# Hybrid decoder block on one core: the test of the largest load is taken early, and the common case follows it

## The chip, the core and the metric

The kernel runs on one core of a Trainium2 chip. The metric is the device time of one execution in microseconds, the median of several runs. The engines are named as in the profile: PE (TensorE) multiplies matrices into PSUM, DVE (VectorE) and ACT (ScalarE) work on vectors, POOL (GpSimd) gathers rows and copies small columns, and SP (SyncE) issues nearly all transfers. Each engine runs its own program; they meet at semaphores.

## The reference

A batch of one with T = 512 tokens of width 1024 goes through one decoder block: a norm, two token mixers (retention and mLSTM) with their projections, an output projection and a residual add, then a hierarchical mixture of experts, a residual add and a last norm. The part around the change is the mixture of experts:

```python
g_w, g_idx = lax.top_k(group_prob, 1)
sel_logits = e_logits[jnp.arange(T), g_idx[:, 0]]
top_logits, e_idx = lax.top_k(sel_logits, TOP_K)          # 2 of the 8 experts of the best of 4 groups
expert_id = g_idx * EXPERTS_PER_GROUP + e_idx             # 32 experts
...
def expert_block(args):
    xb, e = args
    return (jax.nn.silu(xb @ w_gate[e]) * (xb @ w_up[e])) @ w_down[e]
...
return rms_norm(x, norm_final_w)
```

w_gate and w_up are 1024 x 512 and w_down is 512 x 1024 for each expert, all in float32: 6 MB an expert, 192 MB in all. Every weight is read once.

## The kernel before

**Mixer.** The projections are 22 blocks of 512 columns, each of four mix pairs (two slices of 128 rows of the weight), 88 mix pairs in all. ScalarE and VectorE split each weight into a head and a tail (wh, wl, rings of four), and TensorE makes three products of them at line 463. The last two blocks (B_WO) add into the stream x2.

**Router.** After the last block TensorE turns x2 into h2T (turn_stream) and makes the logits (line 608); VectorE picks the experts, and TensorE counts each token's place within its expert (line 624). Then come the tables of moe_round: at16 and at_slot (lines 1449 and 1450) say which token sits in which slot of an expert, the product at line 723 makes the token table (tok_tab), and the product at line 733 the weights by slot (slot_tab, its columns 1 and 2).

**Experts.** The experts are worked on as 16 pairs (PAIRS). One expert has CAP = 64 slots, so that a pair fills the 128 partitions. A pair is: gather its 128 token rows from DRAM (POOL, line 1559, into xg), turn them (turn_x, line 429, then x_copy on VectorE), gate product and up product (gate_or_up, line 650, in two halves each), sigmoid on ScalarE (line 1014), two multiplications on VectorE (lines 1414 and 1419), turn the result (turn_h), down product (down, line 676, two halves), split into yh and yl, and add into x2 by one-hot products (combine, lines 686 and 687, and line 1403). The combine of a pair is spread over the next pair.

**Weights.** A pair's weights come in PAIR_CHUNKS = 12 chunks of 1 MB (gate 4, up 4, down 4), 192 chunks in all, into MOE_RAW = 18 buffers raw_moe, whose places overlay those of the mixer. moe_chunk on SP issues one: after the first 18 it waits until the chunk four before it has landed (IN_FLIGHT, line 360) and until the chunk 18 before it has been used (line 365 for an early half). Chunks 0 to 7 go out during the last mixer blocks, chunks 8 to 15 after the stream's stores (line 400), chunks 16 and 17 after the logits.

**Rounds.** If an expert has more than 64 tokens, further rounds over all pairs are needed. VectorE writes the largest count and the number of extra rounds to cnt. Every engine does pairs 0 to 14 of round 0, then reads cnt, goes through a loop of seven rounds whose body stands in an If and is not taken here, and then does the last pair, number 15 (last_pair(extra) on PE; on SP the last 12 chunks, from LAST_CHUNKS on). On SP it reads

```python
            round_chunks(0)
            sp.wait_ge(cnt_ok, 1)
            most = sp.value_load(cnt[0:1, 0:1], min_val=0, max_val=T)
            with sp.Fori(1, ROUNDS, 1) as r:
                with sp.If(most > r * CAP):
                    round_chunks(r)
            extra = sp.value_load(cnt[0:1, 1:2], min_val=0, max_val=ROUNDS - 1)
            for m in range(LAST_CHUNKS, R_CHUNKS):
                moe_chunk(m, extra, 0, True)
```

at lines 408 to 416. After the last pair come its combine (line 1485 on VectorE), the squares, the last norm (line 1490) and four stores of the output.

Of the kernel before, what the change touches and what calls it, by code (L numbers as in the profile page):

```python
# [68 lines left out]
LAST_CHUNKS = R_CHUNKS - PAIR_CHUNKS  # L69
SP_LOOPS = (LAST_CHUNKS - MOE_RAW) // (2 * MOE_RAW)  # L70
# [23 lines left out]
def hybrid_block(nc, x, norm_mix_w, w_in, ret_gn_w, w_ret, conv_w, conv_b, b_i, b_f, mlstm_gn_w, w_mlstm, w_out,  # L94
                 norm_ffn_w, w_group, b_group, w_router, b_router, w_gate, w_up, w_down, norm_final_w, consts, out):
    ctx = ExitStack()
    with ctx:
# [6 lines left out]
        def sem(name):  # L104
# [27 lines left out]
                   enumerate([64, 72, 0, 8, 16, 24, 80, 88, 32, 40, 48, 56, 96, 104, 112, 120, 144.5, 152.5])]  # L132
# [9 lines left out]
        h2T = at("h2T", 144.5, [P, KD, T])  # L142
# [12 lines left out]
        squares = at("squares", 168.5, [P, TT, D])  # L155
# [19 lines left out]
        def small(name, shape, dt=F32):  # L175
# [64 lines left out]
        at_ok = sem("slots_ready")  # L240
# [21 lines left out]
            "one_hot_ready", "table_in_psum", "table_ready", "counts_ready"))  # L262
# [40 lines left out]
        def _(sp):  # L303
# [72 lines left out]
            def round_chunks(r):  # L376
                if not isinstance(r, int):
                    for m in range(LAST_CHUNKS, R_CHUNKS):
                        moe_chunk(m, r - 1, 0, True)
# [5 lines left out]
                for m in range(MOE_RAW + SP_LOOPS * 2 * MOE_RAW, LAST_CHUNKS):  # L385
                    moe_chunk(m, r, 0, True)
# [27 lines left out]
            extra = sp.value_load(cnt[0:1, 1:2], min_val=0, max_val=ROUNDS - 1)  # L414
            for m in range(LAST_CHUNKS, R_CHUNKS):
                moe_chunk(m, extra, 0, True)
# [9 lines left out]
        def _(pe):  # L426
# [211 lines left out]
            def gate_or_up(r, i, n, up, half):  # L638
# [4 lines left out]
                if half == 0 and (not isinstance(N, int) or N > 0):  # L643
# [19 lines left out]
            def down(r, i, n, half):  # L663

                N, m = r * PAIRS + i * LOOP_PAIRS + n, PAIR_CHUNKS * n + 8 + 2 * half
                if half == 0:
                    pe.wait_ge(hf_ok, N + 1)
                    if not isinstance(N, int) or N > 0:
                        pe.wait_ge(yl_ok, N * 2)
# [44 lines left out]
            def moe_round(r):  # L714
                N0 = r * PAIRS
                if not isinstance(r, int):
                    last_pair(r - 1)
                    combine(N0 - 1, range(8))
# [8 lines left out]

                pe.wait_ge(at_ok, r + 1)
                pe.wait_ge(ww_ok, 1)
                for n in range(2 * TT):  # L730
# [6 lines left out]
                turn_x(N0, 0)  # L737
                turn_x(N0, 1)
                for half in range(2):
                    gate_or_up(r, 0, 0, 0, half)  # L740
                for half in range(2):
                    gate_or_up(r, 0, 0, 1, half)
                turn_x(N0 + 1, 0)
                turn_h(N0)
                down(r, 0, 0, 0)
                turn_x(N0 + 1, 1)
                down(r, 0, 0, 1)
# [32 lines left out]
            N = extra * PAIRS + (PAIRS - 1)  # L780
            pe.wait_ge(c_add, N * 8 + 2)
            pe.wait_ge(oh_ok, N + 1)
            for g in range(8):
                if g < 2:
                    pe.wait_ge(yl_ok, N * 2 + (g + 1))
                    pe.sem_inc(pe_past, 1)
                if g >= 4:
                    pe.wait_ge(fadd, g - 3)
                product((cb[:, 2, :], cb[:, 3, :], pj[:, 0, :], pj[:, 1, :])[g % 4], g).then_inc(fc_ps, 1)
# [3 lines left out]
        def _(act):  # L793
# [191 lines left out]
            def square(t):  # L985
                act.wait_ge(free[t], BLOCKS)
                nc.scalar.activation(squares[:, t, :], x2[:, t, :], ACT.Square, accum_out=ssq[:, t:t + 1]).then_inc(sq_ok, 1)
# [19 lines left out]
            act.wait_ge(e2_ok, 1)  # L1007
            nc.scalar.activation(stat[:, 1, 0:TT], rt[:, 6, 0:TT], ACT.Sigmoid)
# [16 lines left out]
            def moe_round(r):  # L1025
                N0 = r * PAIRS
                if not isinstance(r, int):
                    pair(N0 - 1, last=True)
                pair(N0, first=isinstance(r, int))
                with act.Fori(0, PAIRS - 2, 1) as i:  # L1030
                    pair(N0 + i + 1)

            moe_round(0)
# [22 lines left out]
        def _(dve):  # L1056
# [354 lines left out]
            def pair(N, first=False, last=False, bare=False):  # L1411
# [16 lines left out]
                if first:  # L1428
                    dve.wait_ge(ir_in, 16)
# [6 lines left out]
            def moe_round(r):  # L1436
                N0 = r * PAIRS
                if not isinstance(r, int):

                    pair(N0 - 1, last=True)  # L1440
                    add(N0 - 1, range(8))
# [8 lines left out]
                V.tensor_tensor(at_slot[:, :, :, :].rearrange("p k t s -> p (k t) s"), where, slots, ALU.is_equal).then_inc(at_ok, 1)  # L1450
                if isinstance(r, int):
                    own(V.reduce_max(rt[:, 7, 40:41], cb[:, 1, TT * NE:(TT + 1) * NE], AX.X))
                dve.wait_ge(tab_ps, r * 2 + 2)
                V.tensor_scalar(tok_tab[:, :], cb[:, 2, 0:PAIRS], float(NO_TOKEN), None, ALU.add).then_inc(tab_ok, 1)
                if isinstance(r, int):
                    weights()
                    V.tensor_copy(cnt[:, 0:1], rt[0:1, 7, 40:41])
                    own(V.tensor_scalar(rt[0:1, 7, 48:48 + ROUNDS - 1], kc[0:1, K_LIMIT:K_LIMIT + ROUNDS - 1], rt[0:1, 7, 40:41], None, ALU.is_lt))
                    own(V.reduce_sum(rt[0:1, 7, 41:42], rt[0:1, 7, 48:48 + ROUNDS - 1], AX.X))
                    V.tensor_copy(cnt[:, 1:2], rt[0:1, 7, 41:42]).then_inc(cnt_ok, 1)  # L1460
                V.tensor_scalar(slot_tab[:, :, 0], cb[:, 2, 0:PAIRS], float(NO_TOKEN), None, ALU.add)
                dve.wait_ge(wt_ps, r * 2 + 2)
                V.tensor_copy(slot_tab[:, :, 1:3].rearrange("p n c -> p c n"), cb[:, 3, 0:NE].rearrange("p (c n) -> p c n", c=2)).then_inc(wt_ok, 1)
# [3 lines left out]
                pair(N0, first=isinstance(r, int), bare=True)  # L1467
                with dve.Fori(0, PAIRS - 2, 1) as i:
                    pair(N0 + i + 1)

            moe_round(0)
# [22 lines left out]
        def _(pool):  # L1494
# [52 lines left out]
            def gather(N, n, copies=0):  # L1547

                if not isinstance(N, int) or N > 0:
# [12 lines left out]
            def columns(N, n):  # L1562

                if not isinstance(N, int) or N > 0:
# [5 lines left out]
            def moe_round(r):  # L1570
                N0 = r * PAIRS
                if not isinstance(r, int):
                    columns(N0 - 1, PAIRS - 1)
                pool.wait_ge(tab_ok, r + 1)
                gather(N0, 0)
                gather(N0 + 1, 1)
                pool.wait_ge(wt_ok, r + 1)
                columns(N0, 0)
# [4 lines left out]
            moe_round(0)  # L1583
# [60 lines left out]
```

## Time and profile before

| | |
|---|---|
| median of 3 runs | 1086.86 us (1086.61 to 1087.71) |
| the profiled execution | 1088.14 us, of which the span is 1086.4 |
| mean granted TensorE clock | 0.978 of full |
| busy time: PE, DVE, ACT, POOL | 1013.1, 425.0, 276.6, 70.4 us |
| moved | 263.83 MB, 243 GB/s in the mean |

All positions in the text are microseconds from the start of the span. The page cuts the span into 40 slices of 27.16 us; a stretch view gives for chosen stretches the busy time, the granted clock (1.00 is 2.4 GHz and 0.50 is 1.2 GHz) and the bytes moved. A timeline row gives the start and the length of a group of instructions, and in square brackets how long the engine had been idle and what ended that. The chain of waits is followed back from the last instruction; "issue" in it is time in which the engine waited for nothing that the profile shows. Ends of matmuls are modelled, so a busy TensorE is not one at its peak. SPq is SyncE's queue.

### The profile page before, as it was taken

The page shows a single profiled execution, that of the slowest core. Times are in us where ns is not written, and L with a number is a line of the kernel's source. Part 1 is how long each engine was busy: PE and PEld are TensorE (multiplying, and loading weights), DVE is VectorE, ACT ScalarE, POOL GpSimd, SP SyncE. Part 2 cuts the span into 40 slices and gives each one's busy share as a digit, 9 for nine tenths or more (in the row PEclk, how much of TensorE's full clock was granted, in tenths as well). Part 3 has the DMA queues.
Part 4 walks back from the last instruction along what each step waited for, and adds up shares of the span by engine and source line. Part 5 has one row for each costly group of instructions (what it writes and reads, how often), then busy time and mean ns, then how long its engine had stood idle before and what let it go on. Part 6 is the DMA issues. An engine that isn't in the chain of part 4 may idle for free.

```text
span 1086.4 us, 12967 instructions
## 1 busy us (share of the span) xinstructions
PE 1013.1 (93%) x4661; PEld 649.7 (60%) x4661; DVE 425.0 (39%) x733; ACT 276.6 (25%) x462; POOL 70.4 (6%) x102
## 2 busy tenths in 40 slices
PE   4999999999999999999993999999999999889874
PEld 4888888888888888888883333333333333333322
DVE  4236356434533334535524123333333232333316
ACT  5343564433333336413221000000000000000002
POOL 0564000000000000000000000000000000000000
PEclk9999999999999999999995999999999999999978
DMA  7313222222222222245829799999999999999791
GB/s 273 116 55 141 78 78 78 78 78 78 78 78 78 93 101 79 77 127 171 328 109 395 303 421 420 420 421 421 421 421 420 420 417 421 421 420 418 303 383 78
DMA packets 59959, 263.83 MB, mean 243 GB/s; under 512 B 9152, under 2 KB 9216, under 8 KB 35208
## 3 DMA queue, kind: packets, MB, share of 16 engines
q1 hardware_dynamic: 57432, 257.94, 60.2%
q0 software_dynamic: 2480, 5.26, 1.3%
q8 instruction: 30, 0.49, 0.2%
q14 instruction: 17, 0.14, 0.0%
HBM read 263.17 MB, written 4.20 MB: 246 GB/s over the span
## 4 chain that ended last, share of the span: by engine, by line
PE 55%; DMA 39%; issue 2%; DVE 2%; SPq 1%; ACT 0%; DVEq 0%; POOLq 0%; ACTq 0%
PE pj L463 45%; DMA raw_moe<-in_w_gate_dram 13%; DMA raw_moe<-in_w_up_dram 13%; DMA raw_moe<-in_w_down_dram 12%; PE pj L650 2%; PE cb L429 2%; DMA xg<-x_scratch,tok_tab 1%; PE cb L608 1%; PE cb L482 1%; PE pj L676 1%; PE cb L508 1%; DMA vrow<-in_mlstm_conv_w_dram 1%; PE cb L550 1%; PE cb L512 0%; PE cb L515 0%
## 5 line engine op out<-in xcount | busy, mean ns | idle before, releaser
L650 PE MATMUL pj<-raw_moe,xT 128*64 128x512 f32 x1024 | 233.0, 604 | 25.2 <-issue 10.2
L1070 DVE TENSOR_TENSOR wl<-raw_mix,wh 128x1024 fp32r<-128x1024 f32 x88 | 109.1, 1245 | 183.3 <-ACT wh L807 183.0
L650 PEld LDWEIGHTS pj<-raw_moe,xT 128*64 128x64 f32 x1024 | 75.1, 139 | 168.0 <-issue 168.0
L463 PE MATMUL pj<-wh,hTh 128*128 128x512 f32 x320 | 130.1, 407 | 1.6 <-DVE hTl L1098 1.6
L463 PE MATMUL pj<-wl,hTh 128*128 128x512 f32 x320 | 125.3, 392 | 0.0
L463 PE MATMUL pj<-wh,hTl 128*128 128x512 f32 x320 | 125.0, 391 | 0.0
L807 ACT ACTIVATE wh<-raw_mix 128x1024 fp32r<-128x1024 f32 x88 | 92.4, 1057 | 121.9 <-PE pj L463 111.1
L1403 DVE TENSOR_TENSOR x<-x,cb 128x512 f32<-128x512 f32 x120 | 77.0, 683 | 103.7 <-PE cb L687 103.7
L676 PE MATMUL pj<-raw_moe,hf 128*64 128x512 f32 x512 | 116.7, 598 | 0.8 <-ACT hf L1018 0.8
L463 PE MATMUL pj<-hTh,wh 128*128 128x512 f32 x192 | 80.2, 418 | 0.0
L463 PE MATMUL pj<-hTh,wl 128*128 128x512 f32 x192 | 75.4, 393 | 0.0
L463 PE MATMUL pj<-hTl,wh 128*128 128x512 f32 x192 | 75.1, 391 | 0.0
L676 PEld LDWEIGHTS pj<-raw_moe,hf 128*64 128x64 f32 x512 | 34.2, 136 | 67.0 <-issue 66.8
L463 PEld LDWEIGHTS pj<-wh,hTh 128*128 128x128 f32 x320 | 60.2, 188 | 13.7 <-issue 2.1
L463 PEld LDWEIGHTS pj<-wl,hTh 128*128 128x128 f32 x320 | 60.1, 188 | 13.0
L463 PEld LDWEIGHTS pj<-wh,hTl 128*128 128x128 f32 x320 | 60.3, 188 | 11.8
L1023 ACT ACTIVATE yh<-pj,now 128x512 fp32r<-128x512 f32 x32 | 20.4, 684 | 159.6 <-PE cb L687 143.6
L686 PE MATMUL cb<-yh,hot 128*128 128x512 f32 x124 | 55.0, 444 | 1.3 <-DVE yl L1433 0.8
L1414 DVE SCALAR_TENSOR_TENSOR sg<-pj,now,sg 128x512 f32<-128x512 f32 x16 | 12.0, 751 | 110.0 <-ACT sg L1014 110.0
L687 PE MATMUL cb<-yl,hot 128*128 128x512 f32 x124 | 49.2, 397 | 0.0
L1018 ACT ACTIVATE hf<-cb 128x512 f32<-128x512 f32 x16 | 9.6, 597 | 151.7 <-PE cb L429 151.7
L1408 DVE TENSOR_TENSOR xT<-cb,nwc 128x512 f32<-128x512 f32 x32 | 22.0, 689 | 60.6 <-PE cb L429 60.6
(274 smaller groups left out, 1217.4 us busy)
## 6 DMA issues: line engine op xcount, KB each, us to landing
raw_moe<-in_w_gate_dram SPq DMA_DIRECT2D x64, 1024.0 KB, 9.7
raw_moe<-in_w_up_dram SPq DMA_DIRECT2D x64, 1024.0 KB, 10.1
raw_moe<-in_w_down_dram SPq DMA_DIRECT2D x64, 1024.0 KB, 9.7
raw_mix<-in_w_in_dram SPq DMA_DIRECT2D x32, 1024.0 KB, 5.0
raw_mix<-in_w_ret_branch_dram SPq DMA_DIRECT2D x4, 1024.0 KB, 5.1
raw_mix<-in_w_mlstm_branch_dram SPq DMA_DIRECT2D x4, 1024.0 KB, 5.6
raw_mix<-in_w_out_dram SPq DMA_DIRECT2D x4, 1024.0 KB, 5.2
xt<-in_x_dram SPq DMA_DIRECT2D x4, 512.0 KB, 5.2
```

The source lines that it names most:

```text
L429: return nc.tensor.transpose(o, i, kc[0:k, K_IDENT:K_IDENT + k])
L463: m = nc.tensor.matmul(pj[:, i, :], lhsT, rhs, start=k == 0 and n == 0, stop=k == KD - 1 and n == 2)
L650: mm = nc.tensor.matmul(pj[a * CAP:(a + 1) * CAP, up, :], xT[:, 4 * half + k, a * CAP:(a + 1) * CAP], raw_moe[(m + a) % MOE_RAW][:, k, :], ...
L676: mm = nc.tensor.matmul(pj[a * CAP:(a + 1) * CAP, 2 + c, :], hf[:, 2 * half + f, a * CAP:(a + 1) * CAP], raw_moe[(m + a) % MOE_RAW][:, 2 * ...
L686: nc.tensor.matmul(bank, hot[:, t * P:(t + 1) * P], yh[:, c * 512:(c + 1) * 512], start=True, stop=False)
L687: return nc.tensor.matmul(bank, hot[:, t * P:(t + 1) * P], yl[:, c * 512:(c + 1) * 512], start=False, stop=True)
L807: nc.scalar.activation(wh[:, q % RING, :, :], raw_mix[n % MIX_RAW][:, 2 * (q % 2):2 * (q % 2) + 2, :], ACT.Copy).then_inc(wh_ok, 1)
L1023: nc.scalar.activation(yh[:, c * 512:(c + 1) * 512], pj[:, 2 + c, :], ACT.Copy, scale=now[:, 1:2]).then_inc(yh_ok, 1)
L1070: V.tensor_tensor(wl[:, q % RING, :, :], raw_mix[n % MIX_RAW][:, 2 * (q % 2):2 * (q % 2) + 2, :], wh[:, q % RING, :, :].bitcast(F32), ALU. ...
L1403: V.tensor_tensor(part, part, cb[:, 2 + g % 2, :], ALU.add).then_inc(c_add, 1)
L1408: V.tensor_tensor(xT[:, ks, :], cb[:, part, :].rearrange("p (k n) -> p k n", k=4), nwc[:, ks].unsqueeze(2).to_broadcast([P, 4, P]), ALU.mu ...
L1414: V.scalar_tensor_tensor(sg[:, :], pj[:, 0, :], now[:, 2:3], sg[:, :], ALU.mult, ALU.mult).then_inc(q_ok, 1)
```

## The change

- On every engine all 16 pairs of a round stand together (all_pairs), and the test of the largest count stands ahead of the pairs of round 0: on PE after the token table, the first gather's transposes and the first gate product (first_gate); on DVE after the tables and xT of pair 0; on POOL after the first gather; on ACT ahead of everything of the pairs. On SP all 192 chunks of round 0 are issued first and its test follows them.
- On PE the test is an If with an Else. The common case (largest count at most 64) follows the test at once, with the last sum; further rounds stand in the Else. ACT, DVE and POOL keep the loop of seven rounds with an If, ahead of the last all_pairs(extra).
- cnt is signalled in two steps: the largest count (cnt_ok) ahead of the token table, the number of extra rounds (rounds_ok) after it.
- The weights' table (at_slot, weights(), line 733) comes after the token table and, on PE, after the first gate product and the test.
- The buffers raw_moe are in another order. Chunks 8 and 9 take places of the mixer's raw weights (free once the last tail is made), chunks 10 and 11 places of wh and wl (free after mix pair 85), and all four are issued ahead of the stream's stores. Chunks 12 to 17 follow the stores, without the wait for the logits. h2T moves to 168.5, and squares becomes two tiles of [P, D], with a wait of a square for the one two before it.
- ACT loads the sigmoid table after its test instead of after the router.

```diff
@@ SP @@
+            sp.wait_ge(wl_ok, MIX_PAIRS)
+            moe_chunk(8, 0, 0, False)
+            moe_chunk(9, 0, 0, False)
+            wait_mix_pair(sp, MIX_PAIRS - 3)
+            moe_chunk(10, 0, 0, False)
+            moe_chunk(11, 0, 0, False)
             for t in range(TT):
                 sp.wait_ge(free[t], BLOCKS)
                 sp.dma_start(x_dram[t * P:(t + 1) * P, :], x2[:, t, :]).then_inc(st_in, 16)
-            for m in range(8, 16):
+            for m in range(12, MOE_RAW):
                 moe_chunk(m, 0, 0, False)
...
-            sp.wait_ge(lg_ps, 1)
-            for m in range(16, MOE_RAW):
-                moe_chunk(m, 0, 0, False)
             round_chunks(0)
             sp.wait_ge(cnt_ok, 1)
...
-            extra = sp.value_load(cnt[0:1, 1:2], min_val=0, max_val=ROUNDS - 1)
-            for m in range(LAST_CHUNKS, R_CHUNKS):
-                moe_chunk(m, extra, 0, True)
@@ PE @@
-            moe_round(0)
+            token_table(0)
+            first_gate(0)
             pe.wait_ge(cnt_ok, 1)
             most = pe.value_load(cnt[0:1, 0:1], min_val=0, max_val=T)
-            with pe.Fori(1, ROUNDS, 1) as r:
-                with pe.If(most > r * CAP):
-                    moe_round(r)
-
-            extra = pe.value_load(cnt[0:1, 1:2], min_val=0, max_val=ROUNDS - 1)
-            last_pair(extra)
...
+            with pe.If(most < CAP + 1):
+
+                all_pairs(0)
+                last_sum(PAIRS - 1)
+            with pe.Else():
+                with pe.Fori(1, ROUNDS, 1) as r:
+                    with pe.If(most > r * CAP):
+                        all_pairs(r - 1)
+                        combine(r * PAIRS - 1, range(8))
+                        token_table(r)
+                        first_gate(r)
+                pe.wait_ge(rounds_ok, 1)
+                extra = pe.value_load(cnt[0:1, 1:2], min_val=0, max_val=ROUNDS - 1)
+                all_pairs(extra)
+                last_sum(extra * PAIRS + (PAIRS - 1))
@@ ACT @@
             with act.Fori(1, ROUNDS, 1) as r:
                 with act.If(most > r * CAP):
-                    moe_round(r)
-
-
+                    all_pairs(r - 1)
+            nc.scalar.activation(stat[:, 1, 0:TT], onesq[:, 0:TT], ACT.Sigmoid)
+
+            act.wait_ge(rounds_ok, 1)
             extra = act.value_load(cnt[0:1, 1:2], min_val=0, max_val=ROUNDS - 1)
-            pair(extra * PAIRS + (PAIRS - 1), last=True)
+            all_pairs(extra)
@@ DVE @@
+            tables(0)
+            dve.wait_ge(ir_in, 16)
             most = dve.value_load(cnt[0:1, 0:1], min_val=0, max_val=T)
             with dve.Fori(1, ROUNDS, 1) as r:
                 with dve.If(most > r * CAP):
-                    moe_round(r)
-
+                    all_pairs(r - 1)
+                    add(r * PAIRS - 1, range(8))
+                    tables(r)
 
             extra = dve.value_load(cnt[0:1, 1:2], min_val=0, max_val=ROUNDS - 1)
-            pair(extra * PAIRS + (PAIRS - 1), last=True)
+            all_pairs(extra)
@@ POOL @@
+            first_gather(0)
             pool.wait_ge(cnt_ok, 1)
             most = pool.value_load(cnt[0:1, 0:1], min_val=0, max_val=T)
             with pool.Fori(1, ROUNDS, 1) as r:
                 with pool.If(most > r * CAP):
-                    moe_round(r)
+                    all_pairs(r - 1)
+                    first_gather(r)
+            pool.wait_ge(rounds_ok, 1)
             extra = pool.value_load(cnt[0:1, 1:2], min_val=0, max_val=ROUNDS - 1)
-            columns(extra * PAIRS + (PAIRS - 1), PAIRS - 1)
+            all_pairs(extra)
```

## Rows read from the trace of the kernel before

**Rows 1.** The page, section 2: bytes moved in each of 40 slices.

```profile
GB/s 273 116 55 141 78 78 78 78 78 78 78 78 78 93 101 79 77 127 171 328 109 395 303 421 420 420 421 421 421 421 420 420 417 421 421 420 418 303 383 78
```

**Rows 2.** Experts, 630 to 1000: one stretch (PE busy, clock, DMA, GB/s), then SyncE's waits.

```profile
630.00:1000.00 370.00, 355.47 (x1598) 1.00 1.01 420
...
SPq L360 <- DMA raw_moe<-in_w_gate_dram: 100.4, 51, 2.8
```

**Rows 3.** Stretches around the second hole, columns as in rows 2.

```profile
1017.00:1027.00 10.00, 9.83 (x49) 1.00 0.31 108
1025.00:1027.00 2.00, 2.00 (x12) 1.00 0.43 78
...
1027.00:1056.00 29.00, 18.81 (x74) 0.76 1.01 420
...
1039.27:1045.00 5.73, 5.73 (x14) 0.50 1.01 422
```

**Rows 4.** The chain of waits around SyncE's test: start, length, what.

```profile
1013.42 0.49 SPq L410
...
1014.46 5.26 issue
...
1020.24 0.20 issue
...
1024.07 0.29 SPq L414
...
1025.02 0.35 SPq L373
...
1033.64 5.63 issue
```

**Rows 5.** Timeline of TensorE, pairs 14 and 15.

```profile
1003.18 3.65 PE L650 MATMUL pj<-raw_moe,xT 128*64 128x512 f32 x16 [1.58 <-DMA raw_moe<-in_w_gate_dram]
...
1012.98 3.65 PE L650 MATMUL pj<-raw_moe,xT 128*64 128x512 f32 x16
...
1028.68 0.40 PE L687 MATMUL cb<-yl,hot 128*128 128x512 f32 x1
1039.27 13.39 PE L650 MATMUL pj<-raw_moe,xT 128*64 128x512 f32 x48 [10.19 <-issue]
...
1053.72 3.65 PE L650 MATMUL pj<-raw_moe,xT 128*64 128x512 f32 x16
...
1061.74 7.09 PE L676 MATMUL pj<-raw_moe,hf 128*64 128x512 f32 x32
```

**Rows 6.** The chain of waits ahead of the first pair.

```profile
588.28 8.65 DMA xg<-x_scratch,tok_tab
...
599.04 4.82 PE pj L650 x16
...
604.12 0.36 SPq L373
```

**Rows 7.** Stretches around the first hole, columns as in rows 2.

```profile
585.00:597.00 12.00, 2.52 (x48) 0.50 0.94 380
597.00:606.00 9.00, 8.91 (x36) 0.76 0.16 40
```

**Rows 8.** The gathers, issue to landing: all (view of xg), then the first two (page).

```profile
DMA to landing us min/median/max: 3.3/8.3/8.7
...
xg<-x_scratch,tok_tab POOLq DMA_INDIRECT x2, 6.0
```

**Rows 9.** Timeline of PE, ACT and DVE: slot table, pair 0 and pair 15.

```profile
589.22 1.93 PE L733 MATMUL cb<-wrhot,at_slot 128*64 128x32 f32 x32 [2.27 <-DVE wrhot L1391]
...
607.38 0.69 ACT L1014 ACTIVATE sg<-pj,now 128x512 f32<-128x512 f32 x1 [23.32 <-PE pj L650]
...
1049.29 0.69 ACT L1014 ACTIVATE sg<-pj,now 128x512 f32<-128x512 f32 x1 [18.91 <-PE pj L650]
...
1050.08 0.75 DVE L1414 SCALAR_TENSOR_TENSOR sg<-pj,now,sg 128x512 f32<-128x512 f32 x1 [18.43 <-ACT sg L1014]
```

More of the change, by code:

```diff
@@ L141, in hybrid_block @@
         raw_mix = [at(f"raw_mix{s}", 144.5 + 8 * s, [P, 4, 512]) for s in range(MIX_RAW)]
-        h2T = at("h2T", 144.5, [P, KD, T])
+        h2T = at("h2T", 168.5, [P, KD, T])
         irow = at("irow", 160.5, [P, T])
@@ L154, in hybrid_block @@
         sgm = at("sgm", 168.5, [P, KD, T])
-        squares = at("squares", 168.5, [P, TT, D])
+        squares = [at("squares_even", 184.5, [P, D]), at("squares_odd", 162.5, [P, D])]
         xT = at("xT", 168.5, [P, KD, P])
@@ L384, in round_chunks @@
                         moe_chunk(m, r, i, True)
-                for m in range(MOE_RAW + SP_LOOPS * 2 * MOE_RAW, LAST_CHUNKS):
+                for m in range(MOE_RAW + SP_LOOPS * 2 * MOE_RAW, R_CHUNKS):
                     moe_chunk(m, r, 0, True)
@@ L636, in turn_x, with gate_or_up @@
                 m.then_inc(xT_ps, 1)
-            def gate_or_up(r, i, n, up, half):
+            def gate_or_up(r, i, n, up, half, first=False):
                 N, m = r * PAIRS + i * LOOP_PAIRS + n, PAIR_CHUNKS * n + 4 * up + 2 * half
@@ L642, in gate_or_up @@
                     pe.wait_ge(xT_ok, N * 2 + (half + 1))
-                if half == 0 and (not isinstance(N, int) or N > 0):
+                if half == 0 and not first:
                     pe.wait_ge((q_ok, h_ok)[up], N)
@@ L661, in turn_h, with down @@
                 m.then_inc(ht_ps, 1)
-            def down(r, i, n, half):
+            def down(r, i, n, half, first=False):
                 N, m = r * PAIRS + i * LOOP_PAIRS + n, PAIR_CHUNKS * n + 8 + 2 * half
@@ L667, in down @@
                     pe.wait_ge(hf_ok, N + 1)
-                    if not isinstance(N, int) or N > 0:
+                    if not first:
                         pe.wait_ge(yl_ok, N * 2)
@@ L712, in last_pair, with token_table @@
                 down(r, 0, n, 1)
[L714 to L718, printed above, removed]
+            def token_table(r):
                 pe.wait_ge(hot_ok, r + 1)
@@ L736, in moe_round, with first_gate, all_pairs @@
                             m.then_inc(wt_ps, 1)
-                turn_x(N0, 0)
-                turn_x(N0, 1)
+            def first_gate(r):
+                turn_x(r * PAIRS, 0)
+                turn_x(r * PAIRS, 1)
                 for half in range(2):
-                    gate_or_up(r, 0, 0, 0, half)
+                    gate_or_up(r, 0, 0, 0, half, first=True)
+            def all_pairs(r):
+                N0 = r * PAIRS
+                slot_table(r)
                 for half in range(2):
-                    gate_or_up(r, 0, 0, 1, half)
+                    gate_or_up(r, 0, 0, 1, half, first=True)
                 turn_x(N0 + 1, 0)
                 turn_h(N0)
-                down(r, 0, 0, 0)
+                down(r, 0, 0, 0, first=True)
                 turn_x(N0 + 1, 1)
-                down(r, 0, 0, 1)
+                down(r, 0, 0, 1, first=True)
                 def pair(i, n):
@@ L769, in moe_round, with last_sum @@
                     pair(0, n)
-            moe_round(0)
+                last_pair(r)
+            def last_sum(N):
+                pe.wait_ge(c_add, N * 8 + 2)
+                pe.wait_ge(oh_ok, N + 1)
+                for g in range(8):
+                    if g < 2:
+                        pe.wait_ge(yl_ok, N * 2 + (g + 1))
+                        pe.sem_inc(pe_past, 1)
+                    if g >= 4:
+                        pe.wait_ge(fadd, g - 3)
+                    product((cb[:, 2, :], cb[:, 3, :], pj[:, 0, :], pj[:, 1, :])[g % 4], g).then_inc(fc_ps, 1)
+            token_table(0)
+            first_gate(0)
             pe.wait_ge(cnt_ok, 1)
             most = pe.value_load(cnt[0:1, 0:1], min_val=0, max_val=T)
-            with pe.Fori(1, ROUNDS, 1) as r:
-                with pe.If(most > r * CAP):
-                    moe_round(r)
-            extra = pe.value_load(cnt[0:1, 1:2], min_val=0, max_val=ROUNDS - 1)
-            last_pair(extra)
[L780 to L789, printed above, removed]
+            with pe.If(most < CAP + 1):
[12 more added lines that the diff above has]
+                last_sum(extra * PAIRS + (PAIRS - 1))
         @block.scalar
@@ L1023, in pair, with all_pairs @@
                     nc.scalar.activation(yh[:, c * 512:(c + 1) * 512], pj[:, 2 + c, :], ACT.Copy, scale=now[:, 1:2]).then_inc(yh_ok, 1)
-            def moe_round(r):
+            def all_pairs(r):
                 N0 = r * PAIRS
-                if not isinstance(r, int):
-                    pair(N0 - 1, last=True)
-                pair(N0, first=isinstance(r, int))
+                pair(N0, first=True)
                 with act.Fori(0, PAIRS - 2, 1) as i:
                     pair(N0 + i + 1)
-            moe_round(0)
+                pair(N0 + (PAIRS - 1), last=True)
             act.wait_ge(cnt_ok, 1)
@@ L1409, in x_copy, with pair @@
                                 ALU.mult).then_inc(xT_ok, 1)
-            def pair(N, first=False, last=False, bare=False):
+            def pair(N, last=False, bare=False):
                 dve.wait_ge(now_ok, N + 1)
@@ L1434, in pair, with tables @@
                                            ALU.mult, ALU.subtract).then_inc(yl_ok, 1)
-            def moe_round(r):
+            def tables(r):
                 N0 = r * PAIRS
                 if not isinstance(r, int):
-                    pair(N0 - 1, last=True)
-                    add(N0 - 1, range(8))
                     dve.wait_ge(it_ok, r)
@@ L1449, in moe_round @@
                 V.tensor_tensor(at16[:, :, :, :].rearrange("p k t s -> p (k t) s"), where, slots, ALU.is_equal).then_inc(hot_ok, 1)
-                V.tensor_tensor(at_slot[:, :, :, :].rearrange("p k t s -> p (k t) s"), where, slots, ALU.is_equal).then_inc(at_ok, 1)
                 if isinstance(r, int):
                     own(V.reduce_max(rt[:, 7, 40:41], cb[:, 1, TT * NE:(TT + 1) * NE], AX.X))
+                    V.tensor_copy(cnt[:, 0:1], rt[0:1, 7, 40:41]).then_inc(cnt_ok, 1)
                 dve.wait_ge(tab_ps, r * 2 + 2)
@@ L1545, in _, with gather @@
             pool.wait_ge(zero_ok, 4)
-            def gather(N, n, copies=0):
-                if not isinstance(N, int) or N > 0:
+            def gather(N, n, copies=0, first=False):
+                if not first:
                     pool.wait_ge(xT_ps, N * 2)
@@ L1560, in gather, with columns @@
                                         bounds_check=T - 1, oob_is_err=False).then_inc(gat, 16)
-            def columns(N, n):
-                if not isinstance(N, int) or N > 0:
+            def columns(N, n, first=False):
+                if not first:
                     pool.wait_ge(yl_ok, N * 2)
@@ L1568, in columns, with first_gather, all_pairs @@
                 pool.tensor_copy(now[:, :].unsqueeze(1), slot_tab[:, col, :]).then_inc(now_ok, 1)
-            def moe_round(r):
+            def first_gather(r):
+                pool.wait_ge(tab_ok, r + 1)
+                gather(r * PAIRS, 0, first=True)
+            def all_pairs(r):
                 N0 = r * PAIRS
[L1572 to L1575, printed above, removed]
                 gather(N0 + 1, 1)
                 pool.wait_ge(wt_ok, r + 1)
-                columns(N0, 0)
+                columns(N0, 0, first=True)
                 with pool.Fori(0, PAIRS - 2, 1) as i:
@@ L1581, in moe_round @@
                     columns(N0 + i + 1, i + 1)
-            moe_round(0)
+                columns(N0 + (PAIRS - 1), PAIRS - 1)
+            first_gather(0)
             pool.wait_ge(cnt_ok, 1)
```

38 lines of the change are left out of this document (19 added, 19 removed).

## The prediction, made before the change was run

> **What bounds the kernel now.** I read the page in slices first, then the transfers, then the chain of waits at both ends of the expert stage, and last the order of the engines there. The slice row says that from about 605 us on the core moves 420 GB/s nearly without a break, with one dent in the slice that begins at 1005 us [rows 1]. From 630 to 1000 us the mean is 420 GB/s, and what SyncE's queue waits for there is an earlier weight transfer, not TensorE [rows 2]. So the expert stage is paced by 192 chunks of 1 MB, 18 of them loaded ahead; TensorE keeps up and sits waiting for a chunk before parts of the late pairs [rows 5]. The last instruction can move only if the transfers start earlier, run without a hole, or what follows them gets shorter.
>
> There are two holes. From 597 to 606 us the rate is 40 GB/s: the 18 buffers are full, and nothing has been consumed. The chain there is the first gather (8.65 us), its transposes, the first half of a gate product, and only then the nineteenth chunk at 604.12 [rows 6]. The second hole is from 1017 to 1027 us, 108 GB/s against 420 [rows 3]: 10 x (420 - 108) / 420 = 7.4 us of transfer time are lost. It is SyncE's own. At 1013.42 it turns from the chunks to the load test, and its next chunk goes out at 1025.02 [rows 4]. Of the 11.6 us between, one step of 5.26 us is the first jump over the loop's untaken body; later rounds jump in 0.20 us. TensorE does the same test: its last product of pair 14 starts at 1028.68 and takes 0.40, chunks for pair 15 are there at 1033.64, yet it starts at 1039.27 [rows 4, 5], and it then runs at half clock, granted 0.50 of full (1.2 GHz), until about 1045 [rows 3].
>
> **The change, tail part.** SyncE now issues all 192 chunks and tests afterwards; TensorE tests after its first gate product, so pair 15 follows pair 14 with nothing between. The best measure of such a hand-over is pair 14 itself. Its second gate half starts at 1003.18, as its chunks land [rows 5]. Twelve chunks later means 12 x 1.049 MB / 420 GB/s = 30.0 us, so that pair 15's second gate half starts at 1033.1. (No gather is left in that stretch; with one the period is nearer 30.7, which I keep for the range.) From there to the last up half it is 9.8 us, as in pair 14 (1003.18 to 1012.98). From the last up half to the down product pair 15 takes 1061.74 - 1053.72 = 8.0 us, the same code and combines as before. So the down product starts at 1033.1 + 9.8 + 8.0 = 1050.9 instead of 1061.74. Is its data there? The transfers ended at about 1056.5 and lose the hole of 7.4: 1049.1, in time. Behind the down product nothing changes: 1061.74 to the end of the span, 24.7 us. Gain 10.9 us. The half clock goes with the idle time that preceded it and is within this difference, not on top of it. What is late next is the landing of the last pair's first chunks: TensorE loses the gap and the slow products, but it cannot run ahead of the stream. SyncE's test moves behind its last issue, near 1043, and lasts until about 1055; it is next wanted at the first store, near 1067.
>
> **The front part.** Chunks 8 to 11 move to buffers that are free during the last mixer blocks, when the transfers stand still, and chunks 16 and 17 no longer wait for the logits. Before, ten chunks follow the stream's stores, and the stream is busy until about 596 (the rate of 380 GB/s from 585 to 597 is 11 us at full rate) [rows 7]; four chunks fewer take 4.19 MB / 420 GB/s = 10.0 us from it, so it ends near 586. The gather is issued at 588.28 [rows 6]. In the trace the first gather, into a busy stream, took 8.65 us; its twin, issued at 599.88 into the empty stretch, is the minimum of 3.3 us, since the two of that kind have a median of 6.0 [rows 8] and (8.65 + 3.3) / 2 = 6.0. So I take 3.35: everything after the gather moves 5.3 us earlier, the first gate product from 599.04 to 593.7 and the first refill from 604.12 to 598.8. The bounds are 0 (the gather stays at 8.65) and 5.3. When the gather is issued I leave as it is: VectorE drops at_slot ahead of the token table, but it waits for the table's product anyway.
>
> What is added between the first gate product and the first up product: TensorE's test and the slot table, which stood at 589.22 in idle time, 1.93 us [rows 9]. The trace has no test on TensorE whose start shows. SyncE's, without the jump, is 1013.42 to 1014.46 = 1.04 us [rows 4]; the bounds are 0, hidden behind queued matmuls, and 6.3 with the jump's 5.26. I take 1.04, because the common case is now the code behind the test. Gates then end 8.1 us after their start (599.04 to about 607.1, ahead of the sigmoid at 607.38 [rows 9]), at 601.8; up begins at 604.8 and frees two chunks 3.6 us later, at 608.4. The stream has had four chunks since 600.4 (traffic begins some 1.6 us after the issue, as from 604.12 on) and would run dry at 610.4; with 1.1 us from issue to traffic (1025.02 [rows 4], then a busy share of 0.43 up to 1027 [rows 3]) it has 0.9 us to spare. Cost 0.
>
> VectorE, ScalarE and GpSimd each run the loop of seven untaken branches before pair 0 instead of before pair 15. Bound from SyncE's row, 10.65 us; above it ScalarE's and VectorE's late loops can be no longer than their idle time before 1049 to 1050 (18.9 and 18.4 us [rows 9]), so I take 10.65 and keep 18. ScalarE: 587 to 598, a table load, then ready; its sigmoid is due near 607. GpSimd: the second gather goes out near 601 instead of 594.6, lands by 609, is wanted near 612. VectorE is the tight one: xT copied at 594.5, loop until 605.7 with its last load, then the weight columns and GpSimd's copy of one, both small, for which I allow 1 us, the sigmoid 0.69 and the first multiplication 0.75 [rows 9], ready near 608; the up product ends near 612. Some 3 to 4 us spare, and two more before the stream notices. The other moved pieces (h2T, two small squares tiles with one wait for a square two back, an early sigmoid table) have no consumer near.
>
> **Sum.** 1086.4 - 10.9 - 5.3 = 1070.2 us of span. The profiled execution was 1088.14, 1.74 over its span, and 1.28 over the median of the runs; 1086.86 - 16.2 = 1070.7.
>
> **Rivals.** (a) TensorE's test costs the 5.26 us of a jump after all: up is freed 5.26 us later, less 0.9 of spare: 1075.1. For it: the code behind the test is new to TensorE. Against it: it is the next in line, and no straight stretch in the late pairs shows such a gap. (b) The gather gains nothing, because its 8.65 us were not the stream's doing or because the preload runs on: 1086.86 - 10.9 = 1076.0. Against it stands the twin of 3.3.
> (c) Slower than before: the early loop on VectorE (or GpSimd) pays the first jump's 5.26 us in every round. The absorbed part is 5 us; six more such jumps are 31.6, so 26.6 are lost on the front and the result is 1070.7 + 26.6 = 1097.3. It decides from the second dear jump upward; four more (21 us) eat the whole gain. For it: the loops of these three engines are nowhere visible, and they are exposed only now. Against it: SyncE's loop shows one dear jump only, TensorE's whole gap of 10.2 us [rows 5] has no room for two and the rest, and an all-dear loop (36.8 us) doesn't fit into the 18.4 us that VectorE had.
> What SyncE's row shows is one slow jump, then fast ones. The Trainium skill (Runtime: NRT & Kernel Launch, section Instruction fetch mechanics) says that "a taken branch whose target isn't in the current 2-page window forces a DMA fetch of the target page". By that rule a loop whose head or tail lies across a page edge would refetch in every round, which is the mechanism of (c), and 1097 its price; by SyncE's rows it fetches once. Whether an edge falls so is not to be seen before.
> (d) The change doesn't do what it says at the tail: the last pair's chunks come in time but SyncE's longer straight run or TensorE paces them otherwise, and only the front gains: 1086.86 - 5.3 = 1081.6.
>
> **Chances.** Forecast 0.62, (a) 0.13, (b) 0.12, (c) 0.08, (d) 0.03, and 0.02 for (c) with about four dear jumps, where it comes out even. The range: below, 1067.5, for a first gate half at full clock (2.4 GHz) instead of half and a test that is hidden; above, 1078, past (a) and (b) and a tail period of 30.7. Left out are (c), (d) and a little of the rest. Within 0.2% is about what a measurement of this kernel can tell from no change: faster 0.90, same 0.02, slower 0.08.
>
> **What would show it.** The stream without a dent between 1000 us and its end; the first gather near 3.3 us and the preload over before it is issued; the nineteenth chunk near 599; TensorE at full clock through the last pair, its down product near 1045 or 1046 (1050.9 - 5.3); the last chunk landing near 1044. Wrong would be: a gap of over 3 us between the first gate and the first up product, a hole in the stream near 610, TensorE waiting for VectorE's first inner product, or ScalarE's first sigmoid after 609.

## The result and the profile after

The changed kernel takes 1073.86 us (median of 4 runs, 1071.89 to 1074.01) against 1087.28 us (4 runs, 1086.61 to 1087.78): a ratio of 0.9873 with a 95% interval of 0.9856 to 0.9890. That is 13.4 us faster; forecast were 16.2 and 1070.7 us, with a range of 1067.5 to 1078. The profiled executions are 1088.14 and 1073.83 us, their spans 1086.4 and 1072.0, 14.4 apart. Most of the difference between 13.4 and 14.4 is that the profiled execution of before lay 0.86 us above the median of the four runs, and that of the changed kernel 0.03 below.

First the page of the changed kernel, the span and the bytes moved in 40 slices, which answers to [rows 1]; then stretches (PE busy, clock, DMA share, GB/s) at both holes, which answer to [rows 3, 7].

```profile
span 1072.0 us, 12923 instructions
...
GB/s 276 118 43 156 79 79 79 79 79 79 79 79 79 79 81 116 79 80 167 358 194 336 247 420 419 420 422 421 420 420 421 420 417 421 422 420 420 416 414 91
```

```profile
585.00:597.00 12.00, 4.79 (x30) 0.50 0.12 34
597.00:606.00 9.00, 9.00 (x69) 0.93 0.59 210
...
1000.00:1020.00 20.00, 18.49 (x86) 1.00 1.01 413
1020.00:1040.00 20.00, 18.36 (x80) 1.00 1.01 422
...
1044.00:1046.00 2.00, 1.73 (x7) 1.00 0.62 250
```

The second hole is gone: 413 and 422 GB/s where there were 108, and the granted clock is 1.00 through the last pair. The stream thins out between 1044 and 1046 us, about where its last chunk was forecast (1044). In front the stretch from 585 to 597 us, in which the stream moved 380 GB/s, is now nearly empty (34): the preload is over when the gather is issued, and the idle stretch has moved ahead of it rather than vanished. The chain of waits there answers to [rows 6], start, length, what:

```profile
588.20 4.45 DMA xg<-x_scratch,tok_tab
...
592.79 1.96 PE cb L426 x8
594.77 8.80 PE pj L647 x32
```

And the timelines, in the order SyncE, TensorE, ScalarE, GpSimd and VectorE at the front, then TensorE in the last pair, which answer to [rows 5, 9]:

```profile
600.39 1.07 SPq L372 DMA_DIRECT2D raw_moe<-in_w_up_dram  x2
...
603.35 1.08 PE L728 MATMUL cb<-wrhot,at_slot 128*64 128x32 f32 x32
604.25 7.08 PE L647 MATMUL pj<-raw_moe,xT 128*64 128x512 f32 x32
...
590.49 1.28 ACT L1050 ACT_TABLE_LOAD   x1 [7.95 <-issue]
...
595.62 1.00 POOL L1572 DMA_INDIRECT xg<-x_scratch,tok_tab  x1 [5.99 <-PE cb L426]
...
604.50 0.20 DVE L1476 COPY slot_tab<-cb 128x32 f32<-128x32 f32 x1 [9.02 <-PE cb L728]
605.98 0.75 DVE L1426 SCALAR_TENSOR_TENSOR sg<-pj,now,sg 128x512 f32<-128x512 f32 x1 [1.28 <-ACT sg L1027]
...
1029.01 3.65 PE L647 MATMUL pj<-raw_moe,xT 128*64 128x512 f32 x16 [0.31 <-DMA raw_moe<-in_w_gate_dram]
1033.99 3.65 PE L647 MATMUL pj<-raw_moe,xT 128*64 128x512 f32 x16 [1.32 <-DMA raw_moe<-in_w_up_dram]
...
1038.80 3.65 PE L647 MATMUL pj<-raw_moe,xT 128*64 128x512 f32 x16
...
1046.79 7.09 PE L673 MATMUL pj<-raw_moe,hf 128*64 128x512 f32 x32
```

The first refill goes out at 600.39 instead of 604.12, 3.7 us earlier. The down product of the last pair starts at 1046.79 instead of 1061.74, 14.95 us earlier, so the tail gave 11.2 of them. The span ends 14.4 us earlier; 0.6 us were given back by the last store alone, for which SyncE's queue waited 2.4 us before and 3.0 us after.

### The profile page after: what moved, and what is told of

Same layout as the page of the kernel before. It is cut to its first block, busy times and chain, and to the rows that moved or that the text cites. A ratio compares the mean times of both kernels' runs of the same rounds, so it can differ in the third digit from the quotient of the medians.

```text
span 1072.0 us, 12923 instructions
## 1 busy us (share of the span) xinstructions
PE 1010.2 (94%) x4661; PEld 647.8 (60%) x4661; DVE 425.0 (40%) x733; ACT 276.6 (26%) x462; POOL 70.7 (7%) x102
## 4 chain that ended last, share of the span: by engine, by line
PE 55%; DMA 40%; DVE 2%; issue 1%; SPq 1%; ACT 0%; DVEq 0%; POOLq 0%
PE pj L460 45%; DMA raw_moe<-in_w_up_dram 13%; DMA raw_moe<-in_w_down_dram 13%; DMA raw_moe<-in_w_gate_dram 13%; PE cb L426 2%; PE pj L647 2%; PE cb L605 1%; PE cb L479 1%; PE pj L673 1%; PE cb L505 1%; DMA vrow<-in_mlstm_conv_w_dram 1%; PE cb L547 1%; PE cb L512 0%; PE cb L509 0%; PE cb L486 0%
```

## The experiments

The comparisons are with the changed kernel's 1073.86 us, and each group of runs had the kernel before beside it (medians 1087.49, 1087.71, 1086.98 and 1087.74 us).

**The preload undone.** The order of the buffers, the issues of chunks 8 to 17, h2T and squares as in the kernel before.

```diff
-                   enumerate([64, 72, 0, 8, 16, 24, 80, 88, 144.5, 152.5, 96, 112, 32, 40, 48, 56, 104, 120])]
+                   enumerate([64, 72, 0, 8, 16, 24, 80, 88, 32, 40, 48, 56, 96, 104, 112, 120, 144.5, 152.5])]
...
-            for m in range(12, MOE_RAW):
+            for m in range(8, 16):
                 moe_chunk(m, 0, 0, False)
```

> The changed kernel with the old order of the buffers and the old preload (chunks 8 to 15 after the stream's stores, 16 and 17 after the logits). Theory: the front gain comes from the gather meeting an empty stream; it is back at about 8.6 us, the nineteenth chunk goes out some 4 us later, 1077.9 us (1077 to 1079). Rival: the gather is faster for another reason (the order of the tables and of the products), and the preload is beside the point: 1073.9.

Measured: 1077.62 us (1077.29 to 1078.21). The chain has the long gather again:

```profile
588.86 8.73 DMA xg<-x_scratch,tok_tab
```

So the front is worth 3.8 us, and it comes by the gather meeting an empty stream. The order of the tables and of the products, which this kernel keeps, does not shorten the gather.

**The preload alone, in the kernel before.** The same lines the other way round.

> The kernel before with the new buffers, the new preload, h2T and squares moved, and nothing else. Theory: only the front gain, 1087.3 - 4.0 = 1083.3 us, gather 3.7 to 4.5. The slot table stands here again ahead of the gather. If its activity is what let TensorE's clock rise earlier, the first gate half up to the first refill takes 5.1 us as in the kernel before, not 5.6 as in the changed one. Rival: nothing is gained without the early test, 1087.3.

Measured: 1082.76 us (1082.20 to 1083.29), ratio 0.9956 with an interval of 0.9940 to 0.9973, so 4.7 us. Chain of waits of this kernel:

```profile
588.69 4.13 DMA xg<-x_scratch,tok_tab
...
594.94 5.34 PE pj L653 x16
...
600.53 0.36 SPq L373
```

The two parts nearly add up: 4.7 here and 9.9 for the rest (1087.49 - 1077.62) are 14.6, against 13.4 together. The runs of one kernel lie 1 to 2 us apart, so the 1.2 between these sums is no more than their scatter. The slot table stands ahead of the gather again, and the first refill follows the start of the gate product by 5.59 us, as in the changed kernel (594.77 to 600.39, 5.62) and not as before (599.04 to 604.12, 5.08). The place of the slot table is not what sets the clock there.

**SyncE alone**, in the kernel before; the last 12 chunks behind the loop go with it.

```diff
-SP_LOOPS = (LAST_CHUNKS - MOE_RAW) // (2 * MOE_RAW)
+SP_LOOPS = (R_CHUNKS - MOE_RAW) // (2 * MOE_RAW)
...
-                for m in range(MOE_RAW + SP_LOOPS * 2 * MOE_RAW, LAST_CHUNKS):
+                for m in range(MOE_RAW + SP_LOOPS * 2 * MOE_RAW, R_CHUNKS):
                     moe_chunk(m, r, 0, True)
```

> The kernel before, with SyncE alone issuing all 192 chunks ahead of its test. Theory: the tail needs both engines; the stream ends 7.4 us earlier, but TensorE still starts pair 15 near 1039 and at half clock: 1087.3 us (within 1). Rival: the stream was the bound and its hole the whole tail loss: 1087.3 - 7.4 = 1079.9.

Measured: 1087.68 us (10 runs), ratio 1.0001 (0.9991 to 1.0010). Timeline of its SyncE and TensorE, and the stretch from 1030 to 1040 us:

```profile
1035.28 7.75 SPq L368 DMA_DIRECT2D raw_moe<-in_w_down_dram  x4
...
1039.49 13.00 PE L645 MATMUL pj<-raw_moe,xT 128*64 128x512 f32 x48 [10.53 <-issue]
...
1030.00:1040.00 10.00, 0.51 (x2) 0.54 1.01 416
```

The last four chunks are issued from 1035.28 on, and before from 1041.41 on; the stream has no hole, and nothing is gained. TensorE's own test, 10.53 us of idle time, and the half clock behind it were the limit of the tail all along. The 7.4 us of lost transfer time lay in its shadow.

**SyncE's test back in its old place**, the rest as changed (last 12 chunks behind the loop again).

> The changed kernel with SyncE's test back ahead of the last 12 chunks; the other engines as changed. Theory: the hole of 7.4 us is back in the stream, but TensorE catches up within the last pair, since its first gate half then starts some 5 us late and the rest runs without waits: 2.4 to 2.9 us slower, 1076.6. Rival: the stream sets the end and the whole hole is paid, 1081.3.

Measured: 1077.90 us (1076.80 to 1078.45), 4.0 slower than the changed kernel. Stretch from 1013 to 1023 us, then the last pair's gate product on TensorE, the stretch around it, and the two up halves:

```profile
1013.00:1023.00 10.00, 9.82 (x48) 1.00 0.37 128
...
1028.74 8.64 PE L654 MATMUL pj<-raw_moe,xT 128*64 128x512 f32 x32 [3.37 <-DMA raw_moe<-in_w_gate_dram]
...
1023.00:1040.00 17.00, 12.32 (x49) 0.90 1.00 422
...
1038.68 3.65 PE L654 MATMUL pj<-raw_moe,xT 128*64 128x512 f32 x16 [1.31 <-DMA raw_moe<-in_w_up_dram]
...
1044.06 3.65 PE L654 MATMUL pj<-raw_moe,xT 128*64 128x512 f32 x16 [0.60 <-issue]
```

Nearer to my 2.4 to 2.9 us than to the 7.4 of the rival, but outside both in the medians (the fastest of the four runs is 2.9 above). I had taken the first gate half to start 5 us late and the rest to run without waits. It starts 3.7 us late (1025.05 in the changed kernel), after an idle time of 3.37 us for its chunks, but then nothing is caught up: the gate product runs in part at a lower clock (granted 0.90 in the mean from 1023 to 1040 us, 1.00 in the changed kernel), and the up product waits 1.31 us for its own chunks, as it does in the changed kernel (1.32). So its first half starts 4.7 us late, its second 5.3, and the profiled span is 4.7 longer. With the run before this settles the tail: neither engine's move alone is enough. With SyncE's only, TensorE hides it whole; with TensorE's only, 4.0 us of its gain are missing.

**The common case behind a jump.** TensorE's branches exchanged.

```diff
-            with pe.If(most < CAP + 1):
+            with pe.If(most > CAP):
+                with pe.Fori(1, ROUNDS, 1) as r:
...
+            with pe.Else():
+
                 all_pairs(0)
                 last_sum(PAIRS - 1)
```

> The changed kernel with the two branches of TensorE's test exchanged: further rounds stand behind the test, the common case in the Else, so that it is reached by a far jump. Theory (rival (a) of the prediction): the jump costs up to SyncE's 5.26 us between the first gate product and the slot table, of which the products still queued hide a part and the stream has some 2.7 us to spare (the third pair of refills went out near 608.1 and is needed by about 610.8): 0 to 2.6 us slower, 1073.9 to 1076.5. Rival: the jump is hidden altogether, no gap before the slot table, 1073.9.

Measured: 1073.89 us (1073.76 to 1075.20). Its timeline:

```profile
594.69 8.27 PE L647 MATMUL pj<-raw_moe,xT 128*64 128x512 f32 x32
602.95 1.12 PE L728 MATMUL cb<-wrhot,at_slot 128*64 128x32 f32 x32
```

The slot table follows the gate product without a gap, jump or not. That the common case follows its test at once is worth nothing here: behind 8 us of queued products even the jump is hidden. Two things changed together, though. TensorE's test now stands behind those products, and its path no longer goes through the loop of seven untaken rounds. No run has the loop behind the products, or the test without them, so how the 10.19 us of idle time divide between the two is not shown. The Trainium skill (Advanced Engine Details and Errata, section Engine Queue Depths) gives TensorE a queue of 64 instructions, which is as many as the gate product's 32 matmuls and 32 weight loads. The trace agrees in that there is no gap; no run measures the depth.

**Unused products while TensorE waits**, 40 of them:

```diff
             token_table(0)
+            for _ in range(40):
+                nc.tensor.matmul(cb[:, 3, 0:P], ones16[:, :], hot16[:, :], start=True, stop=True)
             first_gate(0)
```

> The changed kernel with 40 unused products of 128 columns (ones16 by hot16 into the bank of the slot table) between the token table and the first transposes, while TensorE waits for the gather. Theory: the front lost 1.6 us against the forecast in part because the first gate half ran at half clock; with the clock up by then, the transposes and the first half take some 2.3 us less (5.6 to 3.7 and 1.95 to 1.5), the first refill goes out that much earlier and the end with it: 1071.6. Rival: the clock doesn't rise from such products, or what is gained in front is given back by the stream: 1073.9.

Measured: 1074.04 us (1072.04 to 1074.15), no gain. The stretch 597 to 599 us was granted 0.52:

```profile
597.00:599.00 2.00, 2.00 (x8) 0.52 0.35 90
```

**56 of them**, so that they end as the gather lands.

> As the run with 40 unused products, with 56 of them, which at half clock last until the gather lands (586.7 + 56 x 0.107 = 592.7). In the two runs with 40 the clock stood at 0.50 again when the first gate half began, once after having been at 1.00 near 591 to 593 and then fallen in a pause of 1.8 us. Theory: without the pause the clock is up at the first gate half, the first refill goes out near 598.5 instead of 600.4, and the end follows: 1073.9 - 1.9 = 1072.0 us. Rival: the clock's rise near 598 doesn't depend on the products ahead, 1073.9.

Measured: 1072.33 us (1072.00 to 1072.90), 1.5 below the changed kernel. The medians alone do not prove a gain: one of the changed kernel's four runs took 1071.89 us, and the intervals of the two ratios overlap (0.9844 to 0.9877 here, 0.9856 to 0.9890 there). The trace shows how it would come about. Timeline of TensorE and SyncE, and a stretch:

```profile
593.22 1.21 PE L426 MATMUL cb<-kc,xg 128*128 128x128 f32 x8 [1.53 <-DMA xg<-x_scratch,tok_tab]
594.82 7.09 PE L647 MATMUL pj<-raw_moe,xT 128*64 128x512 f32 x32 [0.39 <-DVE xT L1422]
...
598.75 1.07 SPq L372 DMA_DIRECT2D raw_moe<-in_w_up_dram  x2
...
595.00:597.00 2.00, 2.00 (x11) 1.00 0.02 4
```

The first half now takes 3.9 us to its refill (594.82 to 598.75) instead of 5.6, at a clock of 1.00 (2.4 GHz) where the changed kernel had 0.50 (1.2 GHz) until near 598, and the stream and the end of the profiled execution follow (span 1070.5 against 1072.0). So the half clock of the first gate product is a price that can be bought off, 1.7 us of it at the first refill. What it takes is less clear: with the clock up on the way, the 56 ended 1.5 us ahead of the landing after all, and the clock stayed; with 40 it did not rise before 598 in the run above, and in the one below it rose by 591, stood through a pause of 1.8 us and had fallen back by 595. Both versions with 56 products had the clock up for the gate product, neither of the two with 40 did; what decides it is open.

**Tests held back until the gather is done**, alone and with 40 products:

```diff
+            act.wait_ge(gat, 16)
             act.wait_ge(cnt_ok, 1)
...
+            pool.wait_ge(xT_ps, 2)
             pool.wait_ge(cnt_ok, 1)
```

> The changed kernel in which ScalarE waits for the first gather and GpSimd for its transposes ahead of their tests, so that neither tests while the gather runs. Theory: the gather took 4.45 us instead of the 3.3 to 3.7 of its twin because the engines' tests and code loading ran at the same time; it falls to about 3.5, 0.9 us faster, 1073.0. Rival: the first gather is slower for another reason, and the tests are free where they are: 1073.9, or slower if the tests now come too late for the second gather or the first sigmoid.

> Both of the last two edits. If both theories hold the gains add up, 1073.9 - 2.3 - 0.9 = 1070.7 us; if only the clock matters, 1071.6.

Measured: 1074.93 us (1072.56 to 1075.20) and 1074.33 us (1072.42 to 1075.37). First two rows of ScalarE and GpSimd in the first of them, then two stretches of TensorE in the second:

```profile
597.04 1.28 ACT L1051 ACT_TABLE_LOAD   x1 [14.28 <-issue]
...
600.80 1.00 POOL L1573 DMA_INDIRECT xg<-x_scratch,tok_tab  x1 [10.95 <-issue]
...
591.00:593.00 2.00, 0.28 (x6) 1.00 0.28 105
...
595.00:597.00 2.00, 2.00 (x6) 0.50 0.01 4
```

In the first the gather took 4.75 us with no test beside it on ScalarE or GpSimd, so their tests don't slow it. What the first of them gives besides is the price of the loops: ScalarE's table load starts at 597.04, 3.9 us after the gather had landed at 593.17, and GpSimd's second gather at 600.80, 5.5 us after the transposes ended at 595.26. Of these 5.5 the step from the transposes to the gather takes 0.9 without a loop between them too (594.75 to 595.62 in the changed kernel), so that GpSimd's loop is worth about 4.7.

**A gather ahead of the first one**, of row 0 into a spare tile; alone and with the 56 products:

> The changed kernel with an unused indirect gather of the row 0 into a spare tile ahead of the first real one (issued near 578, waited for before the real one). Theory: the first gather of the program takes 4.1 to 4.8 us from issue to landing, and 1.43 us on GpSimd, because it is the first; as the second it takes 3.3 to 3.7 and 1.0 us, 0.9 us faster, 1073.0. Rival: it is slow for another reason, 1073.9; if the unused one, in the busy stream, lands after 587 it delays the real one, 1074 to 1076.

> Both of the last two edits: 1071.1 us if both theories hold, 1072.0 with the clock alone, 1073.0 with the gather alone.

Measured: 1073.78 us (1073.51 to 1074.33) and 1071.89 us (1070.09 to 1073.20). The real gather took 4.83 us in the first, so being the first is not its trouble. The second of them is the fastest version that works on the right rows, ratio 0.9856 to the kernel before (0.9836 to 0.9876); from the one with the 56 products alone (0.9860) it can't be told apart.

**Other rows first.** The first gather takes pair 1's column; pair 0 works on the wrong rows.

```diff
-                gather(r * PAIRS, 0, first=True)
+                gather(r * PAIRS, 1, first=True)
```

> The changed kernel whose first gather takes the token column of pair 1 instead of pair 0 (so pair 0 works on the wrong rows; all instructions and the number of transfers stay). The trace shows 0.29 MB moved by the first gather and 0.18 MB by the second, since empty slots move nothing. Theory: the first gather is slower than its twin because it moves more rows; with the other column it takes 3.7 us instead of 4.45, and the end comes 0.8 us earlier, 1073.1 us. Rival: the length depends on being the first after the stream and the stores, not on the rows, 4.45 and 1073.9.

Measured: 1071.91 us, the median of three runs (1071.26 to 1072.42); a fourth took 5802.65 us, and I have no explanation for it. Below are GpSimd's transfer queue (packets, MB, share) in the changed kernel from 587.5 to 592.6 and from 595 to 600 us, then in this kernel from 587.5 to 593.6 us, and its first gather in the chain:

```profile
q0 software_dynamic: 144, 0.29, 21.4%
...
q0 software_dynamic: 144, 0.18, 14.8%
```

```profile
q0 software_dynamic: 144, 0.18, 11.6%
...
587.74 3.78 DMA xg<-x_scratch,tok_tab
```

With the smaller list the first gather takes 3.78 us, like its twin in the changed kernel (3.7). It is the number of rows, 0.29 MB against 0.18 MB, that the twin of the prediction did not share; 128 rows of 4 kB would be 0.52 MB, so the empty slots move nothing. The 2.0 us below the changed kernel are more than the 0.7 of the gather: the first refill goes out 1.9 us earlier (598.50), of which 0.5 us is an earlier start of the whole front, and 0.8 a first gate half that takes 4.9 us to its refill instead of 5.6, because the clock rose earlier. The code up to there is the same, so I take these two for the scatter between executions.

## Why the prediction was right, and where it was off

**The bound.** Right: transfers pace the experts, and the two holes and their causes were the places. The sum went by TensorE's path, and rightly. What I had read too lightly is the hole: I put its 7.4 us ahead of TensorE's gap, and the run with SyncE alone shows that it cost nothing by itself.

**The tail, 10.9 us.** It measured 11.2, by the same steps: the second gate half of pair 15 starts at 1029.01, 29.8 us after that of pair 14 (999.24), where I had 30.0; 9.8 us to the last up half and 8.0 us to the down product, both as foretold.

**The gather, 5.3 us.** The mechanism held, the size did not: 8.65 to 4.45 is 4.2 us. The term mis-sized is the 3.35 of the twin. It was right that a gather into an empty stream is short, and wrong that the two gathers are alike. The page gives no rows for a gather; the bytes of GpSimd's queue in its stretch would have told. The rows account for 0.7 of the 1.1 us between 3.35 and 4.45 (3.78 with the smaller list). The other 0.4 is in both gathers of the changed kernel: with only the buffers changed they take 4.13 and 3.3 us, in the changed kernel 4.45 and 3.7, for the same bytes. No run shows why.

**The refill, 598.8.** It was 600.39: 1.1 us by the gather, and 0.5 us because the first gate half took 5.6 us where I kept the 5.1 of before. The clock rose near 598.2 (0.50 up to 597, then 0.70 in the mean of 597 to 599), so that 3.4 of the 5.6 us ran at half clock (1.2 GHz); before it rose near 601.4, 2.3 us into the 5.1. I had named the first half's clock only as a chance to be faster. This 0.5 is luck more than a cost of the change: with the code up to there unchanged, the same stretch took 5.1 us in the run with the branches exchanged (594.69 to 599.83), 4.9 in that with two gathers (595.04 to 599.96) and 4.9 in that with other rows first.

**The test and the slot table on TensorE, 1.04 and 1.93 us.** Both too dear: the test is hidden behind queued products, the slot table runs at full clock and delays the up product by 0.9 us (603.35 to 604.25). Neither touched the stream. Rival (a) fell with them. The spare time of the stream there was smaller than forecast: traffic resumes not 1.6 us after the issue at 604.12 but about 0.9 (no transfer up to 605.0, a DMA share of 0.84 behind it), which takes 0.7 from the 0.9 us. Nothing came of it.

**The three early loops, 10.65 us each.** Hidden, as forecast, but for a better reason: 3.9 us on ScalarE (the largest count is written at 586.58, the table load begins at 590.49) and about 4.7 us on GpSimd (from the run with the tests held back; here its second gather follows the transposes by 0.9 us, as before, so the loop was over by then). VectorE's can't be seen: its 9.02 us of idle time ends with the slot table. VectorE's first multiplication starts at 605.98, where I had it end near 608. Rival (c) did not occur; no run puts such a loop where it would repeat a dear jump, so its mechanism stays untested. So does the rule of the Trainium skill (Runtime: NRT & Kernel Launch, Instruction fetch mechanics) that it was named with.

**The sum.** 16.2, less 1.6 in front, plus 0.3 in the tail, less 0.6 at the last store, is the 14.4 us between the spans. The forecast of the median (1070.7 against 1073.86) was 1.4 us further off than that of the span (1070.2 against 1072.0), nearly all of it because I had taken the 1.28 us by which the profiled execution lay above the median of three runs for a constant.

## What to carry to other kernels

A test and its branches cost what stands idle around them. Put them where the engine has work queued in front, as TensorE here, where even a far jump vanishes, or where it would wait anyway, as ScalarE and GpSimd, whose loops of seven untaken rounds cost nothing there. Where two engines pause at the same place, move both: SyncE's move alone gained nothing, though its hole in the profile looked like a loss of 7.4 us, and TensorE's alone fell 4.0 us short. A transfer that the chain waits for should be issued when the stream is empty, and its price read from the bytes that it moves, not from another of its kind.

## What was not expected of the hardware

An engine's loop of seven untaken rounds took 3.9 us on ScalarE and about 4.7 on GpSimd, but 10.65 us on SyncE, half of which is its first jump; ScalarE and GpSimd have far less code in the body. That the size of the body makes the difference is argued, not shown.

Forty products of 128 columns ahead of the work left the clock at 0.50 in one kernel, raised it and lost it again in another; 56 had it at 1.00 for the gate product. A clock of 1.00 at the start of the stage was worth 1.7 us to the first refill (3.9 against 5.6), and the medians at the end lie 1.5 us apart.
